# Modulation in four pieces of shift and scale, with the first two projection tiles run chunk by chunk

## What is computed

```python
x = layer_norm(x, ln0_g, ln0_b)
mod = silu(c) @ ada_w + ada_b                 # c: 1 x 1024, ada_w: 1024 x 6144
sh1, sc1, g1, sh2, sc2, g2 = split(mod, 6)
h = x * (1.0 + sc1) + sh1
z = h @ w_in                                  # 1024 x 1536: pool, recurrent and gate part
y_pool = pool_mixer(z[:, :512])               # windowed means, then a small matmul
y_lru = rglru_mixer(z[:, 512:1024], z[:, 1024:])  # convolution, gates, scan, times gelu
x = layer_norm(ALPHA * x + g1 * (concat(y_pool, y_lru) @ w_out), ln1_g, ln1_b)
h = x * (1.0 + sc2) + sh2
y = peer(h, ...)                              # queries, top-k routing, 16384 experts
x = layer_norm(ALPHA * x + g2 * y, ln2_g, ln2_b)
```

## Time and profile before

| | us |
|---|---|
| median of three runs | 1437.2 (1436.86 to 1437.62) |
| the profiled execution: time | 1438.07 |
| its span in the profile | 1436.3 |
| TensorE busy | 1408.3 (98%) |
| VectorE busy | 1239.4 (86%) |
| ScalarE, GpSimd busy | 589.4 (41%), 570.7 (40%) |
| chain that ended last: TensorE, VectorE | 71%, 24% |

### The profile page before, as it was taken

One profiled execution on the slowest core, in us unless ns is written; L12 is line 12 of the kernel. 1 busy time (PEld: TensorE's weight loads), 2 busy tenths in 40 slices (PEclk: granted clock), 3 DMA queues, 4 the chain that ended last, 5 costly groups with the idle time before them and its releaser, 6 DMA issues.

```text
span 1436.3 us, 20694 instructions
## 1 busy us (share of the span) xinstructions
PE 1408.3 (98%) x7503; PEld 1238.5 (86%) x7503; DVE 1239.4 (86%) x2019; ACT 589.4 (41%) x693; POOL 570.7 (40%) x389
## 2 busy tenths in 40 slices
PE   8999999999998999999999999999999999999997
PEld 7775478899998999998888888888888888888895
DVE  6988969999998999856788888888898888888889
ACT  3561263333334888843333333333333333333331
POOL 0100225549965000001445555454466556664600
PEclk7899999999999999999999999999999999999999
DMA  9924450025464799998999999999999999999961
GB/s 382 328 117 176 146 194 1 1 65 173 162 238 157 259 291 295 287 356 334 369 365 354 372 363 362 370 358 373 355 376 371 362 371 367 381 353 381 357 222 59
DMA packets 159566, 402.34 MB, mean 280 GB/s; under 512 B 11632, under 2 KB 79344, under 8 KB 156432
## 3 DMA queue, kind: packets, MB, share of 16 engines
q1 hardware_dynamic: 120928, 262.17, 51.4%
q0 software_dynamic: 38288, 139.08, 25.7%
q10 hardware_dynamic: 288, 0.29, 0.1%
HBM read 359.56 MB, written 41.94 MB: 280 GB/s over the span
## 4 chain that ended last, share of the span: by engine, by line
PE 71%; DVE 24%; ACT 2%; issue 1%; DMA 1%; SPq 0%; DVEq 0%; ACTq 0%
PE bank L982 21%; PE bank L984 21%; PE bank L983 21%; DVE arena L1597 2%; DVE arena L1589 2%; PE bank L1195 2%; PE bank L1197 2%; DVE arena L1594 1%; DVE arena L1586 1%; DVE arena L1638 1%; DVE arena L1591 1%; DVE arena L1639 1%; PE bank L1071 1%; DVE arena L1635 1%; PE bank L962 1%
## 5 line engine op out<-in xcount | busy, mean ns | idle before, releaser
L982 PE MATMUL bank<-h_lo,u_hi 128*128 128x384 f32 (+1 forms) x1256 | 439.8, 350 | 2.0 <-POOL u_lo L616 1.9
L984 PE MATMUL bank<-h_hi,u_hi 128*128 128x384 f32 (+1 forms) x1256 | 434.6, 346 | 0.0
L983 PE MATMUL bank<-h_hi,u_lo 128*128 128x384 f32 (+1 forms) x1256 | 434.3, 346 | 0.0
L984 PE MATMUL bank<-v_hi,w_hi 128*128 128x512 f32 x744 | 290.9, 391 | 0.0
L983 PE MATMUL bank<-v_hi,w_lo 128*128 128x512 f32 x744 | 290.8, 391 | 0.0
L982 PE MATMUL bank<-v_lo,w_hi 128*128 128x512 f32 x744 | 289.7, 389 | 0.3 <-DVE w_lo L1735 0.3
L982 PEld LDWEIGHTS bank<-h_lo,u_hi 128*128 128x128 f32 x1256 | 236.7, 188 | 13.5 <-ACT arena L819 2.2
L983 PEld LDWEIGHTS bank<-h_hi,u_lo 128*128 128x128 f32 x1256 | 236.7, 188 | 11.2 <-issue 0.5
L876 ACT ACTIVATE v_hi<-v_raw 128x2048 fp32r<-128x2048 f32 x62 | 119.0, 1919 | 307.0 <-PE bank L984 297.2
L984 PEld LDWEIGHTS bank<-h_hi,u_hi 128*128 128x128 f32 x1256 | 236.4, 188 | 9.4
L1729 DVE TENSOR_TENSOR v_lo<-v_raw,v_hi 128x2048 fp32r<-128x2048 f32 x62 | 142.7, 2301 | 105.3 <-ACT v_hi L876 104.5
(11 more groups left out here) (246 smaller groups left out, 1819.8 us busy)
## 6 DMA issues: line engine op xcount, KB each, us to landing
u_raw<-ut_dram SPq DMA_DIRECT2D x128, 512.0 KB, 5.9
v_raw<-v_dram SPq DMA_DIRECT2D x64, 1024.0 KB, 7.3
gate_in<-gates_dram SPq DMA_DIRECT2D x64, 384.0 KB, 7.3
wbuf<-ada_w_dram SPq DMA_DIRECT2D x6, 2048.0 KB, 10.9
early_dram<-arena SPq DMA_DIRECT2D x64, 192.0 KB, 2.3
gates_dram<-wbuf SPq DMA_DIRECT2D x12, 1024.0 KB, 7.3
gates_dram<-arena SPq DMA_DIRECT2D x12, 1024.0 KB, 7.4
w_raw<-early_dram SPq DMA_DIRECT2D x64, 192.0 KB, 5.6
```

The costliest lines, as they stand in the source:

```text
L982: pe.matmul(out, a_hi, b_lo, start=(k == 0), stop=False)
L983: pe.matmul(out, a_lo, b_hi, start=False, stop=False)
L984: return pe.matmul(out, a_hi, b_hi, start=False, stop=(k == n - 1))
```

## The change

The columns of ada_w's first 2048 are put in another order on the host (`pairs`), so that each of the pieces 0 to 3 holds shift and scale of two chunks of h. Scale and bias are made in four parts, each after its piece (`piece_scales`), and z tiles 0 and 1 run two chunks at a time (`first_z`) between the pieces. `BY_VECTOR` is 4. The order and slots of the pieces change; pieces 4 to 8 all go to slot 0, and the gates' tables move to slot 3. VectorE makes the full copy of h for one chunk in place of four, GpSimd makes the low weights of z tiles 0 and 1, the spare matmuls ahead of z are gone. `modulation(4)` and `(5)` move behind z tile 9, and on VectorE `partial_modulation(4)` to `(7)` and `add_gate_row` move to later places.

```diff
-    (("ada", 0), 0), (("ada", 1), 1), (("ada", 2), 2), (("ada", 3), 3),
-    (("win", 1), 0), (("win", 0), 1), (("ada", 4), 2), (("ada", 5), 3), (("win", 2), 2), (("ada", 6), 3),
-    (("wout", 0), 1), (("ada", 7), 3), (("wout", 1), 2), (("ada", 8), 0), (("ada", 9), 3),
+    (("ada", 0), 0), (("win", 1), 3), (("ada", 1), 1), (("ada", 2), 2), (("ada", 3), 0),
+    (("win", 0), 1), (("win", 2), 2), (("ada", 4), 0), (("ada", 5), 0), (("wout", 0), 1), (("ada", 6), 0),
+    (("wout", 1), 2), (("ada", 9), 3), (("ada", 7), 0), (("ada", 8), 0),
-BY_VECTOR = (6, 6, 6, 6)
+BY_VECTOR = (4, 4, 4, 4)
+PER_PIECE = 2
+MOD_BANKS = (7, 6, 7, 6)
+BY_VECTOR_FULL = (6,)
...
-                if (name, j) == ("ada", 8):
+                if (name, j) == ("ada", 9):
                     sp.wait_ge(s_lru, 1)
...
+            for n in range(2):
+                lo_weights(n)
             pool.wait_ge(s_piece[0], 32)
...
-            upper_modulation(0)
-            transposes(0, BANKS_X, range(len(BANKS_X)))
-            modulation(0)
-            upper_modulation(1)
-            modulation(1)
-            upper_modulation(2)
-            modulation(2)
-            upper_modulation(3)
-            modulation(3)
-            spare(SPARE_Z, 0)
...
+            def first_z(j):
+                for n in range(2):
+                    pe.wait_ge(s_wtlo, n + 1)
+                    for k in range(PER_PIECE * j, PER_PIECE * j + PER_PIECE):
+                        pe.wait_ge(s_hlo, k + 1)
+                        z_chunk(n, k)
+            upper_modulation(0)
+            transposes(0, BANKS_H0, range(2))
+            modulation(0)
+            transposes(0, BANKS_H0, range(2, len(BANKS_H0)))
+            for j in range(1, NSPLIT):
+                upper_modulation(j)
+                modulation(j)
+                first_z(j - 1)
+                if len(BANKS_H0) + PER_PIECE * (j - 1) < KD:
+                    transposes(0, BANKS_H0, range(len(BANKS_H0) + PER_PIECE * (j - 1), len(BANKS_H0) + PER_PIECE * j))
+            first_z(NSPLIT - 1)
...
-            z_tiles(2, 5)
-            modulation(4)
-            modulation(5)
-            z_tiles(5, 6)
+            z_tiles(2, 6)
...
-            z_tiles(6, NZ)
+            z_tiles(6, 10)
             pe.wait_ge(s_sig, 8)
+            modulation(4)
+            modulation(5)
+            z_tiles(10, NZ)
...
+            partial_modulation(0, range(BY_VECTOR[0]))
+            piece_scales(0)
+            for j in range(1, NSPLIT):
                 partial_modulation(j, range(BY_VECTOR[j]))
+                low_input(0, BANKS_H0, scale1, bias1, range(PER_PIECE * (j - 1), PER_PIECE * j))
+                piece_scales(j)
+            low_input(0, BANKS_H0, scale1, bias1, range(PER_PIECE * (NSPLIT - 1), KD))
...
             window_sums(0)
             low_weights_of(9)
+            partial_modulation(5)
...
             low_weights_of(11)
+            add_gate_row()
...
-            partial_modulation(7)
+            partial_modulation(6)
...
             affine(0)
             affine(1)
+            partial_modulation(7)
```

More of the change, by code:

```diff
@@ L43 @@
 SPARE_N = 3 * P
-SPARE_FIRST, SPARE_Z, SPARE_Q = 8, 2, 3
+SPARE_FIRST, SPARE_Q = 8, 3
 GATE_PIECES = (4, 5, 10, 11)
@@ L94 @@
 FIN_PARTS = ((slice(0, D),),) * (DENSE - 1) + ((slice(0, D // 2), slice(D // 2, D)),) + ((slice(0, D),),)
+BANKS_H0 = (2, 3, 4, 5)
 BANKS_X = (2, 3, 4, 5, 6)
-Z_LEAD = 4
 BANKS_R = (4, 5, 6, 2, 4, 5, 6, 4)
@@ L232, in build @@
         _, wab, wxb = carve([(AFTER_H,), (4, P), (4, P)])
-        gi, decayed = (wbuf[:, n * 4 * S:(n + 1) * 4 * S].rearrange("p (c n) -> p c n", c=4) for n in range(2))
+        gi, decayed = (wbuf[:, (n + 6) * 4 * S:(n + 7) * 4 * S].rearrange("p (c n) -> p c n", c=4) for n in range(2))
         gr = zx[:, :, PAD_C:]
@@ L372, in weights, with full_by_vector, mod_columns @@
             return piece("wq", h // 2)[:, :, at:at + P]
+        def full_by_vector(stage_of, k):
+            return k % 2 == 0 if stage_of else k in BY_VECTOR_FULL
+        def mod_columns(a):
+            return a.rearrange("p (w k) -> p w k", w=2)
         def of_batch(tables, n):
@@ L394, in _ @@
                     sp.dma_start(piece_buf[:, slot, KD // 2:], src[name][j][:, KD // 2:]).then_inc(s_piece[slot], 16)
+                    if j == NSPLIT - 1:
+                        m, of = SLOT_OF[at_piece[("win", win_order[0])]], src["win"][win_order[0]]
+                        sp.dma_start(piece_buf[:, m, :, 2 * P:], of[:, :, 2 * P:]).then_inc(s_piece[m], 16)
                     continue
@@ L676, in modulate @@
                                    bias=bias[:, k:k + 1], scale=scale[:, k:k + 1]).then_inc(s_hhi, 1)
-                    if k % 2:
+                    if not full_by_vector(stage_of, k):
                         if base + k >= 4:
@@ L945, in modulation, with mod_at @@
                 else:
-                    at = 4 * j + (MOD_UPPER if j < NSPLIT else 0)
                     for m in range(4):
-                        mm = pe.matmul(bank[7][:, at + m:at + m + 1], part[:, j % 2, m * P:(m + 1) * P],
+                        b, at = (MOD_BANKS[j], MOD_UPPER + mod_at(j, m)) if j < NSPLIT else (7, 4 * j + m)
+                        mm = pe.matmul(bank[b][:, at:at + 1], part[:, j % 2, m * P:(m + 1) * P],
                                        ones[:, 0:1], start=True, stop=True)
                 mm.then_inc(s_modmm, 1)
+            def mod_at(j, m):
+                return m // PER_PIECE * KD + j * PER_PIECE + m % PER_PIECE
             def spare(count, b):
@@ L959, in upper_modulation @@
                 wait_piece(pe, "ada", j)
+                if j >= 2:
+                    pe.wait_ge(s_sc, j - 1)
                 for m in range(4):
+                    at = mod_at(j, m)
                     for k in range(BY_VECTOR[j], KD):
-                        pe.matmul(bank[7][:, 4 * j + m:4 * j + m + 1], piece("ada", j)[:, k, m * P:(m + 1) * P],
+                        pe.matmul(bank[MOD_BANKS[j]][:, at:at + 1], piece("ada", j)[:, k, m * P:(m + 1) * P],
                                   silu_c[:, k:k + 1], start=(k == BY_VECTOR[j]), stop=(k == KD - 1))
@@ L1006, in z_chunk @@
                     mm.then_inc(s_zmm, 1)
[L1008 to L1018, removed]
-                z_chunk(1, k)
+            def first_z(j):
[15 more added lines that the diff above has]
+            first_z(NSPLIT - 1)
             def z_tiles(a, b):
@@ L1440, in _ @@
             low_weights_of(4)
-            partial_modulation(5)
             convolve((0, 1))
@@ L1445, in _ @@
             low_weights_of(6)
-            add_gate_row()
             decay_terms(0)
             decay_terms(1)
-            partial_modulation(6)
+            partial_modulation(4)
             low_weights_of(7)
@@ L1927, in pieces, with pairs @@
         return np.ascontiguousarray(w.transpose(2, 1, 0, 3))
+    def pairs(w):
+        w = np.asarray(w)
+        first = np.asarray(w[:, 0:2 * D]).reshape(D, 2, NSPLIT, CHUNK_C // 2).transpose(0, 2, 1, 3).reshape(D, 2 * D)
+        return np.concatenate([first, w[:, 2 * D:]], axis=1)
     cols = np.concatenate([chunks(a) for a in (
@@ L1934 @@
         "x": np.asarray(x)[0], "cols": cols, "rows": rows, "consts": constants(),
-        "ada_w": pieces(ada_w), "w_in": pieces(w_in), "w_out": pieces(w_out), "wq": pieces(peer_wq),
+        "ada_w": pieces(pairs(np.asarray(ada_w).reshape(D, NMOD * D))), "w_in": pieces(w_in), "w_out": pieces(w_out), "wq": pieces(peer_wq),
         "pool_w": np.asarray(pool_w)[0], "wa": np.asarray(lru_wa)[0], "wx": np.asarray(lru_wx)[0],
```

40 lines of the change are left out of this document (22 added, 18 removed).

## The result

| | us |
|---|---|
| before, median of four runs | 1437.03 (1436.53 to 1437.62) |
| after, median of four runs | 1455.79 (1454.42 to 1456.34) |
| ratio | 1.0132, 95% interval 1.012 to 1.0144 |
| profiled execution of after: time, span | 1456.34, 1454.5 |

The change makes the kernel slower by 1.3%. The profiled execution stands 18.3 us over that of before (1438.07), the span 18.2 us. The prediction was 1459.7 with a range of 1444 to 1467.

The account below looks back on a forecast made before the run. It took TensorE's light matmuls, then VectorE's residuals and routing, as the chain, so early delays reach the end in full. 9.0 + 4.0 + 7.5 + 2.0 = +22.5 on 1437.2 gave 1459.7 us, range 1444 to 1467.

Parts of the forecast that it names:

- front: Up to tile 1's eviction: added light matmuls and bursts of z between the pieces end it at 63.6, +9.0 us.
- z stage: VectorE ahead of the pool matmuls: a partial modulation before the gate product, plus gate rows, delays them by 4.0 us.
- mixer: VectorE ahead of the residuals: a 6.0 us step and two landings, less 3.8 us of vanished waits, +7.5 us.
- behind it: Second transposes and first query matmuls: TensorE's gap of some 9 us drops the clock, +2.0 us.
- routing and later: From the routing, where VectorE sets the pace, to the end: the delay passes through in full, nothing added.
- Front, light matmuls: TensorE in the front: 32 more light matmuls, 13.7 us at 1.2 GHz or 7.7 at 2.4; VectorE's relief worth nothing.
- Front, clock: Bursts start at 1.2 GHz, their last three matmuls run at 2.4: 4.5 us, then 7.8 to 7.9 until the next.
- The wait for h: Last burst of the front: it waits for h, whose second chunk comes at 61.2; the burst ends at 63.6.
- The rival of 1466: Front: the clock never returns before the third burst, +15 there, +28.5 in all, 1466 us; chance 0.18.
- faster: light matmuls hidden: Front: light matmuls' weights load under the bursts, cost next to nothing; front -14.7, in all -3.2, 1434 us; chance 0.09.
- the clock stays up: Front: 2.4 GHz from 14.3 us on, -3.4 there, +10.1 in all, 1447 us; chance 0.14.
- VectorE's pieces are covered: Late part: mixer +2.2, z stage 0, no gap for the clock; +11.2 in all, 1448 us; chance 0.07.

Follow-up runs that it names:

- both repairs: The changed kernel with partial modulations 5 and 4 moved earlier and pieces 7, 8 and 9 in slots 3, 0 and 3: 1445.9 us.
- the run with six chunks: The changed kernel with `BY_VECTOR` put back from 4 to 6 for each of the first four pieces: 1444.6 us.
- The run with two slots: The changed kernel with modulation pieces 7, 8 and 9 in slots 3, 0 and 3 in place of 0, 0 and 3: 1449.5 us.
- before with four chunks: The kernel before with `BY_VECTOR` at 4 in place of 6 for each of the first four pieces, nothing else: 1444.7 us.
- the run with more spares: The changed kernel with 15 spare matmuls ahead of the second transposes in place of 3: 1457.3 us.
- the new front with six chunks and the old late part: The changed kernel with `BY_VECTOR` at 6 and everything behind the front put back as before: 1435.1 us, ratio 0.9982.
- piece 1 first: The new front with six chunks and the old late part, with modulation piece 1 issued ahead of the half `win` piece: 1435.8 us, ratio 0.9993.

## Why the prediction held

The sum was right in sign, in size and, but for the front, term by term.

| term | predicted | trace of after |
|---|---|---|
| front | +9.0 | +6.8 |
| z stage | +4.0 | +3.9 |
| mixer | +7.5 | +6.9 |
| behind it | +2.0 | +1.9 |
| routing and later | 0 | -1.3 |
| sum | +22.5 | +18.2 |

*Front, light matmuls.* Right in kind: they stand on the path, do not shrink beside the bursts (16 take 3.63 to 6.83 us), and VectorE's shorter part brings nothing (it waits for TensorE behind each piece). The runs with four and six chunks price them at 8.7 to 9.9 us, between the 7.7 and 13.7 that the prediction gave for all at 2.4 and all at 1.2 GHz.

*Front, clock.* This is the step that failed, in size. The first cycle took as long as worked out: burst at 32.36 (32.1 predicted), next burst at 44.59 (44.4). In part that was luck: only the last matmul of the burst ran at 2.4 GHz, not three, so it took 5.15 us in place of 4.5, and the work behind it made up for that (7.1 in place of 7.8 to 7.9). The prediction then repeated the cycle. In the trace the second burst ended with five matmuls at 2.4 GHz and the clock held through the whole next piece, so the third burst began at 54.09 in place of 56.7. That is 2.6 us; bursts three and four, at 1.2 GHz from 54.4 to 57.8, took 0.4 longer than predicted, and tile 1 came 2.2 us earlier than the 63.6 predicted. The wait for h that the prediction put ahead of the last matmuls does not show. One cycle was taken for all. The five other traces of this front end it at 60.1 to 61.7 too: in four the third burst begins at 2.4 GHz as here, in that of both repairs the second (41.41: 0.49) and not the third (52.68: 0.77). Why it is the one or the other stays open.

The rival of 1466 has the clock return in no burst ahead of the third; it returned in the first already (its last matmul took 0.47 us), and in the second. That a burst starts at 1.2 GHz does not tell it from the forecast, in which every burst starts so. The first two did, and the third began at 2.4 GHz (0.48 us for its first matmul, 0.77 for that of the others). The rule of the Trainium skill named with it, "TensorE: Matmul & The Clock Gate", section "HAM oscillation — how this bites in real kernels", describes two of the bursts of this trace and not the start of the third (it speaks of groups parted by waits; here TensorE was busy between them); in the run with six chunks it fails at the second already (first matmul at 37.85: 0.47).

*z stage.* The gate product was to be 4.3 later than the front makes it and is at 111.52, 10.9 later with a front of 6.8: 4.1. Tile 10's low weights +2.8 (2.9), the pool matmuls +3.9 (4.0). Moving the step away took all of it.

*Mixer.* The waits ahead of 7 and 8 were to be 3.0 and 2.3 and are 3.08 and 2.16; the 3.8 of residual 0 vanished. The run with two slots shows them as the landings' doing: pieces issued one step earlier cost nothing.

*Behind it.* The gap was to be some 9 us without a matmul; TensorE's wait is 7.5, and filling it gave 1.5 us.

*Routing.* The prediction let the delay pass through to the end in full. It did up to the routing, which then took 1.9 us less for a reason that the change doesn't touch (below); 1.0 of this was lost again right behind it, and another 0.3 gained later, of which no row here shows the cause.

The rival "faster: light matmuls hidden" falls with the 0.22 to 0.43 us that each takes in after; "the clock stays up" with the first two bursts at 1.2 GHz; "VectorE's pieces are covered" with the two waits.

## What to carry to other kernels

Ask what an overlap of a dense stage with the light work ahead of it can give back: TensorE lost 2.9 us of spares and a wait of 0.9 there before, the overlap gave 2 to 3 us, and the matmuls of one column that came with it cost 9 to 10. A transfer that must wait for its forerunner's buffer puts its landing (here some 7.8 us) behind the consumer's step, and what the consumer has no other work for is lost; look for the pair of slots that lets the next piece be on its way. A step that is moved from an engine's idle stretch to a place on the path costs its duration less the waits that it fills there, whatever the total busy time says: 7.3 us of steps cost 3.9 in the z stage and one of 6.0 some 2 in the mixer, though VectorE was busy for 9 us less after the change.

## What the runs showed of the hardware

**The routing has lengths that don't belong to its code.** From its first maximum to the reciprocal behind the last head it took 235.6 to 235.8 us in before and in five other traces, and 231.7 to 233.8 in the other seven, with the same instructions. The time goes in steps of VectorE that meet a step of GpSimd. The same two steps, in before and then in after:

```profile
369.88 1.52 DVE L1616 TENSOR_TENSOR arena<-arena 128x256 f32<-128x256 f32 x1
371.32 1.45 DVE L1619 TENSOR_TENSOR arena<-arena 128x192 f32<-128x192 f32 x1
```

```profile
389.33 0.42 DVE L1648 TENSOR_TENSOR arena<-arena 128x256 f32<-128x256 f32 x1
389.66 0.35 DVE L1651 TENSOR_TENSOR arena<-arena 128x192 f32<-128x192 f32 x1
```

GpSimd at the same places:

```profile
368.58 2.54 POOL L616 TENSOR_TENSOR u_lo<-u_raw,u_hi 128x512 fp32r<-128x512 f32 x2
371.08 1.47 POOL L569 TENSOR_TENSOR xt<-xt,row_b 128x512 f32<-128x512 f32 x1
```

```profile
388.02 1.29 POOL L582 TENSOR_TENSOR xt<-xt,row_b 128x512 f32<-128x512 f32 x1
389.68 2.73 POOL L631 TENSOR_TENSOR u_lo<-u_raw,u_hi 128x512 fp32r<-128x512 f32 x2 [0.37 <-ACT u_hi L825]
```

Before, each of the two steps began inside a GpSimd step and ended 0.2 to 0.3 us behind it, 1.1 us longer than in after, where the first began in the 0.37 us in which GpSimd stood still. The h step of 2.11 us above shows the same, for a step of 0.69; GpSimd's two low weights beside it took 5.24 us, and 4.64 in the run without that edit. The Trainium skill, "SBUF — State Buffer", section "Who interferes with whom", says that a VectorE instruction with two inputs in SBUF contends with a GpSimd instruction that reads SBUF, and that the one that comes second is blocked entirely; these rows agree with it.

All six long routings have these two steps at 1.5 and 1.4 us; of the short ones six have both at 0.3 to 0.4, and the shortest (before with four chunks) has the second at 1.44. Laid side by side step for step, the routings of before and after part at three more places: a copy (377.68 in before), 0.3 us longer in before, a comparison (384.69), 1.1 shorter, and a cast (402.54), 0.45 longer. At each a GpSimd step was running when the longer one began. The five make up 1.9 us, nearly the whole difference; the copy and the cast have one input, of which the sentence above does not speak. What sets the phase of the two engines was not tried and stays open.

Half of the difference reaches TensorE. The long routings end in a wait of 3.6 us of TensorE for which the profile names no releaser, the short ones in one of 0.4 to 0.5. The kernel lets TensorE wait there for the routing's weights, and in all 13 traces its first matmul starts 0.1 us after the step of VectorE that makes them ends (457.24 and 457.13 in before), so VectorE is the releaser, as the prediction read it. That start comes 240.1 us after the first maximum in before and 239.2 in after, since behind the routing a product takes 0.69 us in before and 1.65 in after, beside a GpSimd step again. For such a kernel it means that an edit of 1 to 2 us ahead of the routing can be given back in part or added to by it, as in the run with more spares.

**Some versions vary more from run to run.** Before stayed within 3.1 us in 21 runs; the new front with six chunks and the old late part spread over 7.3 us in 11, but with piece 1 first it stayed within 2.8 us in 11, and the old front with four chunks spread over 4.6 us in four. So the new front alone does not make the spread, and what does is not shown. The front's end differs from trace to trace with where the clock falls: 16 light matmuls of the first piece took 3.63 us in one trace and 4.68 in another of the same front.
